# Attention work of a hybrid transformer block regrouped: logits of four jobs at once, placed with the value products between two token tiles, and query and key turning moved from TensorE to DMA transposes

## The chip, the cores and the metric

The program runs on one core of one Trainium2 chip. The metric is the device time of one execution in microseconds (us), taken as the median of several; lower is better.

## The reference, cut to what matters

One layer on 256 tokens of width 1024, all in float32: a mixer with three attention branches, then a SwiGLU FFN.

```python
h, mem_n = rms_norm(x, pre_mix_g), rms_norm(mem, mem_norm_g)
(q_n, k_c, v_c, k_s, v_s, k_w, v_w, g_n, q_m, k_m, v_m, q_x,
 gate_nsa, gate_moba, gate_mem) = split_columns(h @ w_in)          # 2328 + 3 x 1024 columns
# NSA, 8 heads of 64 in 2 groups: keys compressed to 15, "selected" blocks, a window, each gated
o_nsa = gb[..., 0:1] * o_c + gb[..., 1:2] * o_s + gb[..., 2:3] * o_w
o_m = moba_attention(q_m, k_m, v_m, rel_bias)                      # 4 heads, causal
o_x = memory_attention(q_x, *split(mem_n @ w_mem_kv))              # 4 heads into 256 memory tokens
merged = (sigmoid(gate_nsa) * (o_nsa @ w_nsa_o) + sigmoid(gate_moba) * (o_m @ w_moba_o)
          + sigmoid(gate_mem) * (o_x @ w_mem_o))
x = x + rms_norm(merged @ w_mix_out, post_mix_g)
h = rms_norm(x, pre_ffn_g)
x = x + rms_norm((silu(h @ w_ffn_gate) * (h @ w_ffn_up)) @ w_ffn_down, post_ffn_g)
```

At 256 tokens every selected block is chosen, so the selected and the window branch are both causal attention with their own keys. That makes 4 MoBA heads, 4 memory heads, 8 selected and 8 window heads: 24 score matrices of 256 x 256, of which all but the memory ones are causal (the first token tile sees 128 keys, the second 256).

## The kernel before

**Projections.** Tokens lie in two tiles t = 0 and 1 of 128. A weight matrix comes in by parts of 256 rows x 512 columns, numbered v. SyncE loads units of two parts into four `raw` buffers; ScalarE (ACT) rounds a part into `wh` (L577, counted by `hi_done`), VectorE (DVE) takes the rest into `wl` (L888, `lo_done`), and TensorE (PE) multiplies it in `sub`: for each t, for each of two 128-row halves, three matmuls of 512 columns (L1271, L1272, L1273: high x high, high x low, low x high), 12 in all. Four parts make a block b, which accumulates in one half of the PSUM tile `acc` (b % 2). Before a block begins, `free_acc(b)` waits until both token tiles of block b - 2 have been read out: `ev[0]` and `ev[1]` at b - 1 or more, increments that come block by block.

**Front.** Blocks 0 to 5 give queries, keys and values (`pat`), and the memory's (`kvm`). Matmuls need queries and keys with the head dimension on partitions, so `qk_batch` turns four 128 x 128 tiles by TensorE transposes (L1384) into a PSUM bank, and ACT copies the bank out (`evac_qk`, L664). There are eight batches: 0 is the input of the compression, 1 to 3 the NSA queries and keys, 4 and 5 MoBA's, 6 the memory keys, 7 the memory queries (in slot 0). They stand between parts of blocks 2 to 5.

**Attention.** Slots n = 0 to 27 follow, one part v = V_GATE + n of a gate or output projection each, so that the projection covers the attention. Slots 0 to 15 hold gate blocks 6 to 9; slots 16 and 17 are blocks 10 and 11 (MoBA's output projection, one part each); slots 18 to 21 are block 12; slots 22 and 23 are blocks 13 and 14 (the memory's); slots 24 to 27 are block 15. The 24 jobs are n = 0 to 3 MoBA, 4 to 7 memory, then by fours selected, selected, window, window for heads i and 4 + i. A job goes through all engines:

- PE, `scores(n)` (L1464) at the start of an even slot: logits of jobs n and n + 1, one on array rows 0 to 63, the other on rows 64 to 127, in float32 (two records per matmul), into two of three banks.
- DVE: bias added (L1105), row maxima (L1113), `x_done` (L1115).
- ACT: `exp` with the sum (L761), `e_done`. DVE: reciprocal (L1125), `r_done`.
- GpSimd (POOL): scales the job in `sx` (L529), splits it into 16-bit halves `pplanes` (L535). `sx` and `pplanes` hold two jobs each.
- SP: `cross_probs(n)` turns them by a DMA transpose (L440) into `pcrossed`, also two jobs deep (it waits for `joined`). ACT: `join` (L738) in slot n + 3 puts the halves together.
- PE, `values(g)` (L1504): four joined jobs times values into bank `ob`, at the end of slots 7, 11, 15, 19, 23 and 27, so right ahead of the next `scores`. ACT then takes `ob` to `oh` (L745) and DVE the rest to `ol` (L1142).

ACT and DVE run a written order. In slot n, ACT does: high part of v = V_GATE + n + 5 or so, exp of job n, `join(n - 3)`, `oh`, and where a gate block has ended its read-out (`evac_gate`, L723; block 12's is in its slot 21). DVE does: maxima of job n, then the read-out of an output block (`merge`, L1079; block 10 in its slot 17, block 13 in its slot 23), the low part, the reciprocal of job n, `ol`. Slot 4 also holds four TensorE transposes of the compressed probabilities (L1525), which ACT copies to `pct` (L752).

After slot 27 come the NSA projection (blocks 16, 17), the mix, and 11 FFN blocks and the down projection, which the change leaves alone.

## Time and profile before

| | |
|---|---|
| median of 3 runs | 402.14 us (401.96 to 402.21) |
| profiled execution, its own time | 402.37 us |
| its span (first to last instruction) | 400.6 us |
| PE, DVE, ACT, POOL busy | 98%, 66%, 61%, 24% |
| attention slots 0 to 27 | from 77 to 179 us of the span |

Times in rows are microseconds from the start of the span, unless marked ns. Durations of matmuls are modelled latencies that overlap; the distance from the start of one to the start of the next is the cost. PE is TensorE's matmuls, SPq the issue of a DMA by SyncE.

### The profile page before, as it was taken

What the parts mean: (1) busy time and instruction counts of PE and PEld (TensorE: products, weight loads), DVE (VectorE), ACT (ScalarE), POOL (GpSimd) and SP (SyncE); (2) the same over time, 40 slices, a digit from 0 to 9 for tenths busy, and PEclk for the clock granted to TensorE, in tenths of its full rate; (3) what the DMA queues carried; (4) which work ended last, traced back from release to release, by engine and by line L of the source; (5) the groups of instructions that cost most, each with busy time, mean ns of one, the idle gap of its engine ahead of it and who ended that gap; (6) DMA issues with size and microseconds to landing.
All of it is one profiled execution on the core that took longest, in us unless ns stands there. A gap on an engine that the chain in (4) does not pass through costs nothing.

```text
span 400.6 us, 5611 instructions
## 1 busy us (share of the span) xinstructions
PE 392.8 (98%) x1950; PEld 315.9 (79%) x1950; DVE 264.8 (66%) x438; ACT 244.3 (61%) x410; POOL 94.3 (24%) x127
## 2 busy tenths in 40 slices
PE   8999999999999999999999999999999999999994
PEld 5788888877777777778888888888888888888883
DVE  4876764897697898957769673566556566556424
ACT  5675673559999988755548853545554546444422
POOL 3100010045856455310000032133333321210000
PEclk9999999999999999999999999999999999999998
DMA  8999994655998978968564584677778777865002
GB/s 284 392 378 393 317 369 164 211 144 147 236 306 196 239 165 200 230 214 290 184 209 153 192 259 131 211 204 199 213 222 236 231 191 183 222 224 207 2 1 105
DMA packets 84784, 86.68 MB, mean 216 GB/s; under 512 B 33948, under 2 KB 61128, under 8 KB 84760
## 3 DMA queue, kind: packets, MB, share of 16 engines
q1 hardware_dynamic: 83384, 83.49, 69.9%
q0 software_dynamic: 800, 2.33, 1.7%
q10 hardware_dynamic: 576, 0.56, 0.4%
q8 instruction: 13, 0.21, 0.2%
q14 instruction: 11, 0.09, 0.1%
HBM read 77.43 MB, written 1.07 MB: 196 GB/s over the span
## 4 chain that ended last, share of the span: by engine, by line
PE 88%; ACT 3%; DVE 3%; issue 2%; POOL 2%; DMA 1%; DVEq 0%; ACTq 0%; SPq 0%; POOLq 0%
PE acc L1271 25%; PE acc L1273 25%; PE acc L1272 25%; PE ob L1504 2%; DMA gates<-pplanes 1%; PE ptb L1434 1%; PE acc L1316 1%; ACT sx L761 1%; PE acc L1312 1%; PE acc L1575 1%; PE acc L1576 1%; PE acc L1317 1%; PE acc L1581 1%; POOL pplanes L535 1%; ACT pts L738 1%
## 5 line engine op out<-in xcount | busy, mean ns | idle before, releaser
L888 DVE TENSOR_TENSOR wl<-raw,wh 128x1024 fp32r<-128x1024 f32 (+1 forms) x126 | 159.0, 1271 | 84.5 <-ACT wh L577 84.0
L577 ACT ACTIVATE wh<-raw 128x1024 fp32r<-128x1024 f32 (+1 forms) x126 | 130.1, 1044 | 68.9 <-PE acc L1273 66.1
L1271 PE MATMUL acc<-wh,xlh 128*128 128x512 f32 (+1 forms) x352 | 137.5, 391 | 0.0
L1273 PE MATMUL acc<-wh,xlh 128*128 128x512 f32 (+1 forms) x352 | 135.5, 385 | 0.0
L1272 PE MATMUL acc<-wl,xlh 128*128 128x512 f32 (+1 forms) x352 | 135.5, 385 | 0.0
L1271 PEld LDWEIGHTS acc<-wh,xlh 128*128 128x128 f32 x352 | 66.1, 188 | 15.8 <-issue 3.2
L1273 PEld LDWEIGHTS acc<-wh,xlh 128*128 128x128 f32 x352 | 66.1, 188 | 13.4
L1272 PEld LDWEIGHTS acc<-wl,xlh 128*128 128x128 f32 x352 | 66.1, 188 | 12.5
L555 POOL COPY at<-crossed 128x512 uint16<-128x512 uint16 x22 | 22.8, 1084 | 80.8 <-DMA crossed<-planes 80.8
L1271 PE MATMUL acc<-wh,ah 128*128 128x512 f32 x88 | 34.2, 389 | 0.0
L1272 PE MATMUL acc<-wl,ah 128*128 128x512 f32 x88 | 34.2, 389 | 0.0
L1273 PE MATMUL acc<-wh,al 128*128 128x512 f32 x88 | 34.2, 389 | 0.0
L535 POOL COPY pplanes<-sx 128x768 uint16<-128x768 uint16 (+1 forms) x24 | 25.4, 1056 | 8.0 <-DMA gates<-pplanes 7.0
L761 ACT ACTIVATE sx<-sx,jst 128x128 f32<-128x128 f32 (+1 forms) x40 | 17.9, 448 | 8.1 <-DVE jst L1115 7.7
L837 ACT ACTIVATE glu<-acc,rstd 128x256 f32<-128x256 f32 x22 | 10.4, 475 | 16.5 <-PE acc L1273 16.5
L529 POOL TENSOR_SCALAR sx<-sx,jst,gsig 128x128 f32<-128x128 f32 (+1 forms) x32 | 15.8, 505 | 19.3 <-DVE jst L1125 19.3
L1271 PEld LDWEIGHTS acc<-wh,ah 128*128 128x128 f32 x88 | 16.5, 188 | 3.5
L1272 PEld LDWEIGHTS acc<-wl,ah 128*128 128x128 f32 x88 | 16.5, 188 | 3.5
L1273 PEld LDWEIGHTS acc<-wh,al 128*128 128x128 f32 x88 | 16.5, 188 | 3.4
L738 ACT ACTIVATE pts<-gates 128x768 uint16<-128x768 uint16 (+1 forms) x16 | 17.7, 1109 | 0.0
L550 POOL COPY planes<-glu 128x1024 uint16<-128x1024 uint16 x11 | 12.4, 1125 | 20.0 <-DVE glu L1220 20.0
L529 POOL TENSOR_SCALAR sx<-sx,jst 128x256 f32<-128x256 f32 (+1 forms) x16 | 10.2, 649 | 29.1 <-DVE jst L1125 29.1
(198 smaller groups left out, 444.8 us busy)
## 6 DMA issues: line engine op xcount, KB each, us to landing
raw<-in_w_in SPq DMA_DIRECT2D x18, 1024.0 KB
raw<-in_w_ffn_gate SPq DMA_DIRECT2D x22, 512.0 KB
raw<-in_w_ffn_up SPq DMA_DIRECT2D x22, 512.0 KB
raw<-in_w_ffn_down SPq DMA_DIRECT2D x22, 512.0 KB
raw<-in_w_mix_out SPq DMA_DIRECT2D x4, 1024.0 KB
raw<-in_w_mem_kv SPq DMA_DIRECT2D x2, 1024.0 KB
raw<-in_w_nsa_o SPq DMA_DIRECT2D x2, 1024.0 KB
tb<-g_scratch SPq DMA_DIRECT2D x1, 1536.0 KB, 11.2
```

The source lines that it names most:

```text
L529: ins = nc.gpsimd.tensor_scalar(probs, probs, jst[:, 3, n, t:t + 1], branch_gate, ALU.mult, ALU.mult)
L535: nc.gpsimd.tensor_copy(pplanes[:, n % 2, 0:2 * w].rearrange("p (h c) -> p h c", h=2), sx[:, n % 2, 0:w].bitcast(U16).rearrange("p (c h) - ...
L550: nc.gpsimd.tensor_copy(planes[:], act_tok.bitcast(U16).rearrange("p t (n h) -> p h t n", h=2)).then_inc(planes_done, 1)
L555: ins = nc.gpsimd.tensor_copy(at[:, j].bitcast(U16).rearrange("p f (t n h) -> p h t f n", t=TILES, h=2)[:, h], crossed[:, h])
L577: nc.scalar.activation(wh[:, k, :, 0:w], raw_part(slot, part)[:, :, 0:w], ACT.Copy).then_inc(hi_done, 1)
L738: ins = nc.scalar.activation(dst.bitcast(U16).rearrange("p (c h) -> p h c", h=2), src, ACT.Copy)
L761: ins = nc.scalar.activation(probs, src, ACT.Exp, bias=jst[:, 1, n, t:t + 1], scale=SCALE, accum_out=jst[:, 2, n, t:t + 1])
L837: nc.scalar.activation(silu[:, t], acc[:, j, t, 0:GU_W], ACT.Silu, scale=rstd[:, 3, t:t + 1]).then_inc(silu_done, 1)
L888: nc.vector.tensor_tensor(wl[:, k, :, 0:w], raw_part(slot, part)[:, :, 0:w], wh[:, k, :, 0:w].bitcast(F32), ALU.subtract).then_inc(lo_done, 1)
L1271: nc.tensor.matmul(bank[:, 0:w], h[:, k, c], wh[:, slot, s, 0:w], start=first, stop=False)
L1272: nc.tensor.matmul(bank[:, 0:w], h[:, k, c], wl[:, slot, s, 0:w], start=False, stop=False)
L1273: return nc.tensor.matmul(bank[:, 0:w], l[:, k, c], wh[:, slot, s, 0:w], start=False, stop=last)
```

## The change

1. Query and key tiles of batches 1, 2, 3, 6 and 7 (now `QK_PAIRS` k = 0 to 4), and the compressed probabilities (`CMP_TURN`, k = 5), are no longer turned by TensorE. POOL splits a pair of tiles into 16-bit halves (`split_qk`), SP turns them by a DMA transpose (`cross_qk`), POOL joins them with two copies (`join_qk`). ACT's copies out of PSUM for them are gone. The batch of the compression (`compress_turn`) and MoBA's two (`moba_turn`) stay on TensorE.
2. Logits come for four jobs at once (`group_scores`), except for the memory jobs, which keep pairs (`pair_scores`). For the NSA groups one matmul takes selected and window keys together, 256 or 512 columns wide. The t = 0 logits of four jobs lie in bank 2, the t = 1 logits in banks 0 and 1. Row halves 0 and 1 of the array do unlike tiles at a time.
3. `values(g)` and `group_scores(n)` stand after the t = 0 matmuls of the part in slots 0, 8, 12, 16, 20 (values alone in slot 24), in place of the end or start of slots. The last `values` stays after slot 27.
4. `sx` becomes a ring of four (two of them in `gates`); ACT's exp and DVE's bias addition wait for POOL's split of job n - 4. DVE computes maxima of job n + 1 in slot n, after the reciprocal, except for the first job of a group. ACT's and DVE's read-out of `ob` moves to slots 8, 12, ..., 24.

The diff, cut to its core:

```diff
+QK_PAIRS = [("q", Q_NSA), ("q", Q_NSA + 2), ("k", K_SEL), ("k", K_MEM), ("q", Q_MEM)]
+QK_READY = [1, 1, 3, 5, 6]
+QK_NSA_Q, QK_ALL = 2, 5
...
+def values_group(slot):
+    if slot == JOBS + VALUE_LAG - 1:
+        return JOBS // 4 - 1
+    return slot // 4 - 2 if slot % 4 == 0 and slot >= 8 else None
...
@@ SP
+            def cross_qk(k):
+                sp.wait_ge(qk_split, k + 1)
+                sp.dma_start_transpose(qk_buffers[QK_BUFFER[k]][1].rearrange("p (b n) -> p b n", n=P),
+                                       qk_buffers[QK_BUFFER[k]][0]).then_inc(qk_turned[QK_BUFFER[k]], 16)
...
             projection(3)
+            cross_qk(0)
+            cross_qk(1)
...
             sp.dma_start(tb[:], ...)
+            cross_qk(2)
             for u in range(2 * B_GATE, 2 * B_GATE + 5):
                 mix_unit(u)
+                if u >= 15:
+                    cross_qk(u - 12)
             cross_probs(0)
             mix_unit(17)
             cross_probs(1)
             cross_probs(2)
+            cross_qk(CMP_TURN)
...
@@ POOL
+            split_qk(0)
+            split_qk(1)
+            pool.wait_ge(cmp_in_done, 1)
             nc.gpsimd.memset(vcz, 0.0).then_inc(zeroed, 1)
+            join_qk(0)
+            join_qk(1)
+            split_qk(2)
             pool.wait_ge(tb_d, 16)
...
+            join_qk(2)
+            pool.wait_ge(mq_pe, 2)
             nc.gpsimd.memset(pcz, 0.0).then_inc(zeroed, 1)
+            split_qk(3)
+            split_qk(4)
+            join_qk(3)
             for n, (kind, *_r) in enumerate(jobs):
+                if n == CMP_SLOT - 2:
+                    join_qk(4)
+                if n == CMP_SLOT - 1:
+                    split_qk(CMP_TURN)
+                if n == CMP_SLOT + 2:
+                    join_qk(CMP_TURN)
                 pool.wait_ge(r_done, n + 1)
...
@@ DVE
             for n in range(JOBS + VALUE_LAG):
+                if n < JOBS and (n % 4 == 0 or in_pairs(n) and n % 2 == 0):
+                    row_maxima(n)
...
                     nc.vector.reciprocal(jst[:, 3, n, :], jst[:, 2, n, :]).then_inc(r_done, 1)
+                    if n % 2 == 0 or n % 4 == 1 and not in_pairs(n):
+                        row_maxima(n + 1)
...
@@ PE
+            def group_scores(n):
+                if n == 0:
+                    pe.wait_ge(mq_ev, 2)
+                    pe.wait_ge(cmp_read, 1)
+                elif in_pairs(n - 1):
+                    pe.wait_ge(e_done, n)
+                else:
+                    pe.wait_ge(x_done, n)
+                if n == 0:
+                    steps = [(0, 0), (1, 1), (2, 0), (3, 1), (0, 1), (1, 0), (2, 1), (3, 0)]
+                    for i, (j, t) in enumerate(steps):
+                        if i == 5:
+                            pe.wait_ge(even_firsts, 1)
+                        ins = logits_of(n + j, t)
+                        if i == 2:
+                            ins.then_inc(even_firsts, 1)
+                else:
+                    logits_of(n, 0, keys=2).then_inc(even_firsts, 1)
+                    logits_of(n + 1, 1, keys=2)
+                    logits_of(n, 1, keys=2)
+                    pe.wait_ge(even_firsts, n // 4)
+                    ins = logits_of(n + 1, 0, keys=2)
                 ins.then_inc(s_done, 1)
...
             for n in range(JOBS + VALUE_LAG):
-                if n < JOBS and n % 2 == 0:
-                    scores(n)
-                if n == CMP_SLOT:
...
+                if in_pairs(n) and n % 2 == 0:
+                    pair_scores(n)
+                def attention(n=n):
+                    g = values_group(n)
+                    if g is not None and n < JOBS + VALUE_LAG - 1:
+                        values(g)
+                    if n < JOBS and n % 4 == 0 and not in_pairs(n):
+                        group_scores(n)
...
-                    gate_sub(n)
-                if n == 0:
-                    qk_batch(QK_LAST, 6, [col(C_QX), col(C_QX + P)])
-                if n >= VALUE_LAG + 3 and n % 4 == 3:
-                    values((n - VALUE_LAG - 3) // 4)
+                    gate_sub(n, attention)
+                if n == JOBS + VALUE_LAG - 1:
+                    values(JOBS // 4 - 1)
```

`pair_scores(4)` waits for `qk_joined` at 5 and `x_done` at 4, `pair_scores(6)` for `e_done` at 5; `compressed_scores` waits for `qk_joined` at 2.

## Rows read from the trace of the kernel before

**Rows 1.** The page: busy time of each engine, and the granted TensorE clock by slices.
```profile
PE 392.8 (98%) x1950; PEld 315.9 (79%) x1950; DVE 264.8 (66%) x438; ACT 244.3 (61%) x410; POOL 94.3 (24%) x127
...
PEclk9999999999999999999999999999999999999998
```

**Rows 2.** Windows: start:end, length, busy of each engine, PEclk, DMA share, GB/s.
```profile
30.00:54.00 24.00, 24.00 (x115) 19.85 (x114) 17.21 (x24) 15.81 (x26) 0.53 (x1) 1.00 1.06 356
98.00:106.00 8.00, 7.51 (x48) 5.80 (x47) 6.16 (x11) 7.90 (x19) 7.82 (x7) 1.00 0.92 211
```

**Rows 3.** Timeline of PE around batch 2: start, duration, engine, line, operation.
```profile
37.73 0.39 PE L1273 MATMUL acc<-wh,xlh 128*128 128x512 f32 x1
37.96 0.60 PE L1384 MATMUL sbank<-const,pat 128*128 128x128 f32 x4
38.31 0.48 PE L1271 MATMUL acc<-wh,xlh 128*128 128x512 f32 x1
38.63 0.40 PE L1272 MATMUL acc<-wl,xlh 128*128 128x512 f32 x1
```

**Rows 4.** Timeline of PE around `scores(2)`.
```profile
82.69 0.39 PE L1273 MATMUL acc<-wh,xlh 128*128 128x512 f32 x1
83.01 0.37 PE L1464 MATMUL ptb<-kt,qt 64*128 64x128 f32 x1
83.02 0.37 PE L1464 MATMUL sbank<-kt,qt 64*128 64x128 f32 x1
...
83.34 0.38 PE L1464 MATMUL ptb<-kt,qt 64*128 64x256 f32 x1
...
83.56 0.38 PE L1464 MATMUL ptb<-kt,qt 64*128 64x256 f32 x1
...
83.87 0.50 PE L1271 MATMUL acc<-wh,xlh 128*128 128x512 f32 x1
84.20 0.39 PE L1272 MATMUL acc<-wl,xlh 128*128 128x512 f32 x1
```

**Rows 5.** Timeline of PE: the transposes of slot 4, behind scores.
```profile
90.60 0.66 PE L1525 MATMUL ob<-const,pat 128*128 128x128 f32 x4
91.02 0.48 PE L1271 MATMUL acc<-wh,xlh 128*128 128x512 f32 x1
```

**Rows 6.** Timeline of PE: the last product, then `values(0)`; the same, then `values(1)`.
```profile
103.05 0.39 PE L1273 MATMUL acc<-wh,xlh 128*128 128x512 f32 x1
103.93 1.52 PE L1504 MATMUL ob<-pts,pat 128*64 128x256 f32 x16 [0.49 <-issue]
...
118.11 0.39 PE L1273 MATMUL acc<-wh,xlh 128*128 128x512 f32 x1
119.07 1.08 PE L1504 MATMUL ob<-pat,kvm 128*64 128x256 f32 x8 [0.57 <-ACT pts L738]
```

**Rows 7.** Timeline of PE and DVE after `scores(16)`.
```profile
136.73 0.50 PE L1271 MATMUL acc<-wh,oh 128*128 128x512 f32 x1
...
136.85 0.62 DVE L1105 TENSOR_TENSOR sx<-sbank,tb 128x128 f32<-128x128 f32 x2
...
140.97 1.28 DVE L1079 SCALAR_TENSOR_TENSOR gates<-gates,acc 128x512 f32<-128x512 f32 x2
```

**Rows 8.** Timeline of PE, ACT and DVE after `scores(20)`.
```profile
151.66 0.50 PE L1271 MATMUL acc<-wh,xlh 128*128 128x512 f32 x1
...
157.77 1.25 ACT L723 ACTIVATE gates<-acc,rstd 128x512 f32<-128x512 f32 x2
...
162.47 1.28 DVE L1079 SCALAR_TENSOR_TENSOR gates<-gates,acc 128x512 f32<-128x512 f32 x2
```

**Rows 9.** One line each: durations in ns, and landing of the transposes, min/median/max.
```profile
L555 POOL COPY at<-crossed x22: 763/777/1743, 237.5 to 352.3; 128x512 uint16<-128x512 uint16 x22
...
DMA to landing us min/median/max: 2.7/4.2/6.5
```

**Rows 10.** The line of POOL that splits jobs: durations in ns, min/median/max.
```profile
L535 POOL COPY pplanes<-sx x24: 824/825/1974, 81.2 to 166.6; 128x768 uint16<-128x768 uint16 x20, 128x1024 uint16<-128x1024 uint16 x4
```

More of the change, by code:

```diff
@@ L102, in job_plan, with in_pairs, sx_place, sx_user @@
     return jobs
+def in_pairs(job):
+    return MOBA_H <= job < MOBA_H + MEM_H
+def sx_place(job):
+    return job % 4 if job < JOBS - 2 else job % 2
+def sx_user(job):
+    return job - 4 if job < JOBS - 2 else job - 2
+def logits_count(job):
+    g = job // 4
+    return 1 if g == 0 else 2 + job % 4 // 2 if g == 1 else g + 2
 def ends_group(job):
@@ L242, in build_layer @@
             jst = sb("jst", [P, 5, JOBS, TILES], F32, s)
+            with ExitStack() as early:
+                front = sb("front", [P, 2, 1024], U16, early)
+            qk_buffers = [(front[:, 0], front[:, 1]),
+                          tuple(pts[:, j].rearrange("p t q -> p (t q)").bitcast(U16) for j in (2, 3)),
+                          tuple(gates[:, j, 5 * SLICE:6 * SLICE].bitcast(U16) for j in range(2))]
+            sx_ring = [sx[:, 0], sx[:, 1], gates[:, 0, 0:SLICE], gates[:, 1, 0:SLICE]]
             pplanes = sb("pplanes", [P, 2, 1024], U16, s)
@@ new lines, in row_maxima @@
+            def row_maxima(n):
+                kind, h, _q, _k, bh = jobs[n]
+                dve.wait_ge(s_done, logits_count(n))
+                if kind == "mem":
+                    bank = score_banks[n % 4 % 3]
+                    link(nc.vector.tensor_reduce(jst[:, 0, n, :], bank.rearrange("p (t k) -> p t k", t=2), AX, ALU.max))
+                else:
+                    if n >= 4:
+                        dve.wait_ge(pplanes_done, sx_user(n) + 1)
+                    for t in range(TILES):
+                        c0, c1 = prob_cols(kind, t)
+                        nc.vector.tensor_tensor(prob_view(n, kind, t), logits(n, t), tb[:, bh, c1 - c0 - 1::-1],
+                                ALU.add).then_inc(dve_c, 1)
+                        chain[0] += 1
+                    dve.wait_ge(dve_c, chain[0] - 1)
+                    for t in range(TILES):
+                        if t == 1:
+                            dve.wait_ge(dve_c, chain[0])
+                        ins = nc.vector.reduce_max(jst[:, 0, n, t:t + 1], prob_view(n, kind, t), axis=AX)
+                    link(ins)
+                nc.vector.tensor_scalar(jst[:, 1, n, :], jst[:, 0, n, :], -SCALE, None, ALU.mult).then_inc(x_done, 1)
@@ L1451, in scores, with logits_of @@
-            def scores(n):
-                if n == 0:
-                    pe.wait_ge(qk_ev[1], 3)
-                    pe.wait_ge(qk_ev[0], 4)
-                elif jobs[n - 2][0] == "mem":
+                        after={0: [lambda: moba_turn(0)], 1: [lambda: moba_turn(1)], 2: [compress_1], 3: [add_column_groups]})
+            whole_block(B_TAIL, 20, 4, xh, xl, w=ATT_TAIL, after={1: [compress_2], 3: [compressed_scores]})
+            def logits_of(n, t, keys=1):
+                _kind, _h, q, k, _bh = jobs[n]
+                rows, dst = half_rows(n % 2), logits(n, t)
+                count = dst.shape[1]
+                if keys == 2:
+                    c = 256 * (n % 2) if t == 0 else 0
+                    dst = score_banks[2 if t == 0 else n % 2][:, c:c + 2 * count].rearrange("p (a c) -> p a c", a=2)
+                    return nc.tensor.matmul(dst, qt[rows, q, P * t:P * t + P], kt[rows, k:k + 2, 0:count], start=True, stop=True)
+                return nc.tensor.matmul(dst, qt[rows, q, P * t:P * t + P], kt[rows, k, 0:count], start=True, stop=True)
@@ L1457, in scores, with pair_scores @@
+            def pair_scores(n):
+                if n == MOBA_H:
+                    pe.wait_ge(qk_joined, QK_ALL)
+                    pe.wait_ge(x_done, n)
+                else:
                     pe.wait_ge(e_done, n - 1)
-                else:
-                    pe.wait_ge(x_done, n - 1)
                 for t in range(TILES):
                     for side in range(2):
-                        kind, _h, q, k, _bh = jobs[n + side]
-                        c0, c1 = prob_cols(kind, t)
-                        ins = nc.tensor.matmul(score_banks[(n + side) % 3][:, c0:c1], qt[half_rows(side), q, P * t:P * t + P],
-                                               kt[half_rows(side), k, 0:c1 - c0], start=True, stop=True)
+                        ins = logits_of(n + side, t)
+                ins.then_inc(s_done, 1)
@@ L1488, in values @@
                 pe.wait_ge(joined, 4 * g + 4)
-                if g == 0:
-                    pe.wait_ge(te_done, 1)
+                if jobs[4 * g][0] == "sel":
+                    pe.wait_ge(qk_joined, CMP_TURN + 1)
                 sides = [[], []]
```

205 lines of the change are left out of this document (100 added, 105 removed).

## The prediction, written before the run

> **What bounds the kernel now.** I read the page first, then the timeline of PE, then the order of DVE and ACT in the attention slots. The page shows PE busy 98% of the span at the full granted clock, the other engines at most 66% [rows 1]. So a thing that leaves PE's queue is worth its time, as long as nothing else makes PE wait. Busy time of PE hides short waits, since the durations are latencies that overlap. I therefore measure from start to start: products follow each other every 0.23 us [rows 3], and whatever widens that distance is a cost.
>
> Three costs show. Four transposes between products: 38.63 - 37.73 less two pitches of 0.23 is 0.44 us [rows 3]. A pair of logits by the same sum: 84.20 - 82.69 - 0.46 = 1.05 us, of which entering takes 0.32 - 0.23 = 0.09, the products behind it come 0.11 late, and the rest is from 83.01 to 83.87 [rows 4]. Last, waits at `values`: its first record comes 0.88 us behind the last product for group 0 and 0.96 for group 1 [rows 6], against 0.32 for an entry that waits for nothing [rows 4], so 0.56 + 0.64 = 1.20 us are stall. In that stretch ACT is busy 7.90 of 8 us and POOL 7.82 [rows 2]: the chain over the other engines is late there, not PE.
>
> **What leaves PE.** (a) Transposes. Batches 1, 2, 3 and 7 stand alone: 4 x 0.44 = 1.76 us. Batch 6 shares its excursion with `compress_2` and slot 4's with scores; four transposes are 0.42 us there [rows 5], so 0.84. Sum 2.60.
>
> (b) Grouping. A 256-column record pair takes 83.56 - 83.34 = 0.22 us a record [rows 4]; two records of it and two half as wide make 0.64 us for a pair of jobs of 128 + 256 columns, the rest of the 1.05 is entry, exit and fill, 0.41. Four jobs have twice the columns: 1.28 + 0.41 = 1.69 us alone. Wide matmuls with two keys have the same columns. Slots 10, 14, 18 and 22 lose an excursion of 1.05, and 0.64 of it returns in the group ahead (which stands behind `values` before and after): 4 x 0.41 = 1.64. MoBA's two pairs cost 0.86 (scores 0 shares an excursion with the compressed scores, so only 83.87 - 83.01) + 1.05 = 1.91, its group 1.69: 0.22. Memory pairs stay. Sum 1.86.
>
> (c) Stalls of `values` 0 and 1: they come 6 products or 1.4 us later in PE's order, and the jobs come earlier, since DVE does the maxima of job n + 1 in slot n, `sx` is four deep, and ACT loses the copy of batch 7 and of `pct`. I take the whole 1.20. With none of it the gain is 1.2 less; that is the lower end of this term.
>
> Together 2.60 + 1.86 + 1.20 = 5.66 us.
>
> **What PE meets in place of it.** In DVE's order nothing of slot n goes ahead of the maxima of a group's first job, and they need `s_done`. After that moment DVE and ACT need a fixed time for what lies in their queues, and some of it is what `free_acc` waits for. The trace shows these times, and the change shortens PE's way to those waits.
>
> - Slot 18 (block 12) waits for `merge` of block 10, in DVE's slot 17: queued ahead of it are the maxima of 16, a low part, the reciprocal, the maxima of 17. Before, PE's next product after scores(16) is at 136.73 and the merge ends at 140.97 + 1.28 = 142.25, 5.5 us later [rows 7]. PE had the whole of slots 16 and 17 and a pair of logits to do until then and lost nothing. After, only 6 + 12 products lie between: 18 x 0.23 + 0.11 = 4.25 us. Stall 1.3 us.
> - Slot 23 (block 14) waits for ACT's read-out of block 12 in its slot 21, behind exp 20, join 17, `oh`, a high part, exp 21 and join 18: it ends at 157.77 + 1.25 = 159.02, 7.4 us after 151.66 [rows 8]. PE is there after 30 products, 7.0 us. Stall 0.4 us.
> - Slot 24 (block 15) waits for `merge` of block 13, DVE's slot 23, behind exp 22 on ACT and the maxima of 23: 162.47 + 1.28 = 163.75, 12.1 us after 151.66 [rows 8]. PE is there 7.4 + 12 x 0.23 = 10.1 us after. Before, scores(22) and `values(4)` (now inside slot 24, behind the wait) filled this time. Stall 2.0 us.
>
> Sum 3.7 us. Behind a stalled `free_acc` stand all later products; the high and low parts are several parts ahead, so nothing else is late. The stalls don't pay each other back: each is counted from its own `s_done`. Had DVE and ACT been quicker by 2 us everywhere, nearly all would vanish, so the term runs from 0 to 3.7; three POOL clashes of 0.7 us more (below) give 5.8.
>
> **What the other queues get.** POOL gets six splits and six joins. A join is two copies like those of L555, 0.78 us each, 1.74 at most [rows 9], so 1.6 to 3.5 us; a split of 1024 half-words is like L535's, 0.8 to 2.0 us [rows 10]. Most lie where POOL does little (0.53 of 24 us in the windows [rows 2]). The tight one is `join_qk(4)`: it stands ahead of job 2 on POOL, and `pair_scores(4)` on PE waits for it. From the end of MoBA's group PE has 42 products, 9.7 us, to go to it. In that time DVE does the maxima of jobs 0 and 1 and a low part, ACT two exps, POOL scales and splits jobs 0 and 1 (before, a job took it 1.8 us) and joins: about 6.8 + 1.6 = 8.4 us as an estimate, or 9.7 and more if low parts of DVE get in first. So 0 to 1 us of stall, I take 0.3. `join_qk(5)` delays jobs 6 and 7, which `values(1)` needs; laying the same durations end to end, they are joined less than 1 us ahead of PE, an estimate with no margin to speak of. POOL's longest splits take 1.97 us against a median of 0.83 [rows 10]. The Trainium skill ("SBUF — State Buffer", Who interferes with whom) says that a VectorE instruction with two SBUF inputs and a GpSimd instruction that reads SBUF shut each other out for a whole instruction, the later one waiting; the trace agrees with its 1.97 against 0.83, and by it each clash costs up to one low part on either side.
>
> SP issues `cross_qk(0)` and `(1)` behind part 7's load, with DMA at a share of 1.06 [rows 2], so loads for blocks 4 and 5 land later by two issues and two turns, an estimate of 5 us from landings of 2.7 to 6.5 us [rows 9]. The rounding of those parts runs 4 us or more ahead of PE. Cost 0; if that cover is gone, 1 to 2 us. ACT only loses work in front.
>
> **The sum.** 5.66 - 3.7 - 0.3 = 1.7 us. The profiled execution took 402.37 (span 400.6 and 1.8 around it), which gives 400.7; it lies 0.2 above the median of 402.14, which gives 400.4.
>
> **The rivals.** They and my forecast share 100.
>
> 1. Stalls don't appear (18): the read-outs are earlier, the gain is 4.5 to 5.6 and the time 396.5 to 397.6. For it: the ring of four frees DVE and ACT from POOL. Against: both long chains are ACT's and DVE's own work after `s_done`, as measured.
> 2. Tiles of unlike length on the two row halves do not run side by side (8): slower. Before, both halves start together (83.01 and 83.02 [rows 4]) but always with equal columns; the groups set 256 columns beside 512. Run one by one the four matmuls take 2.56 us in place of 1.28, in five groups 6.4 us: 5.66 - 3.7 - 6.4 = -4.4, so 406.6. It decides from 0.35 us lost a group. The Trainium skill ("TensorE: Matmul & The Clock Gate", The mechanism) says that matmuls keep program order in start and in end, and tiles on other row groups still overlap. By that rule the written order, short, long, long, short, would still overlap in full, and the sum stays; if order also held each matmul's two records together, part of the 6.4 would come.
> 3. POOL and the turns become the bound of slots 4 to 12 (18): `qk_joined`, `joined` 4 or 8 come late, PE keeps its stalls at `values` and gets new ones of 1 to 2 us. Gain 1.7 - 1.2 - 1.5 = -1.0, so 401 to 403.5. For it: POOL 7.82 of 8 us busy before it got more. Against: all jobs start their chain with PE further behind them.
> 4. Turns starve the front of weights (4): 402 to 404.
>
> My forecast has 52.
>
> **How the numbers follow.** A measurement of this kernel can tell about 0.2% (0.8 us) from no change. Within my case, 399.0 to 401.8, some 8 of 52 are above 401.3. Faster: 44 + 18 = 62. Same: 8 + 8 of rival 3. Slower: 10 + 8 + 4 = 22. The range leaves out rival 2, the lowest of rival 1 and the highest of 3 and 4: 397.2 to 403.2.
>
> **What would show it.** Distances between products at former batches 1, 2, 3 and 7 of 0.23; `values` 0 and 1 entered 0.32 behind a product; the group's records from first to last about 1.3 us; PE records pausing before slots 18, 23 and 24 by 1.3, 0.4 and 2.0 us, with `merge` ending 5.5 and 12.1 us after the group. It is wrong if those pauses are missing (faster), if the group takes over 1.6 us, or if PE pauses at `pair_scores(4)` or `values(1)` (slower).

## The result, and the profile after

The changed kernel takes 402.89 us, the median of 6 runs (402.24 to 404.13); the kernel before, on the same chip, takes 402.17 (401.96 to 402.64, 6 runs). The ratio is 1.0022, with an interval of 1.0012 to 1.0031: slower by 0.2%. I had predicted 400.4. The profiled execution took 402.24 with a span of 400.4 us, which makes it the fastest of the six; before, the profiled one had a span of 400.6.

The page of the kernel after, in the lines of [rows 1]:

```profile
PE 388.7 (97%) x1894; PEld 314.1 (78%) x1894; DVE 266.7 (67%) x438; ACT 240.3 (60%) x404; POOL 121.5 (30%) x146
...
PEclk9999999999999999999999999999999999999998
```

PE has 56 records fewer and 4.1 us less of busy time, and the span is 0.2 us shorter. So the work did leave PE, and something made PE wait for as long. POOL has 27 us more. The windows of [rows 2] for the kernel after (start:end, length, busy of each engine, PEclk, DMA share, GB/s):

```profile
30.00:54.00 24.00, 24.00 (x112) 19.88 (x111) 19.65 (x26) 13.93 (x23) 7.01 (x7) 1.00 1.08 315
98.00:106.00 8.00, 8.00 (x48) 5.96 (x47) 5.12 (x9) 7.07 (x16) 7.87 (x9) 1.00 0.88 208
```

In the second stretch, which holds `values(0)` in both kernels, ACT and DVE got free by about a microsecond each; POOL is as full as before. Where PE waited, in the list of its waits from 30 to 200 us (in all, how often, longest):

```profile
PE acc L1380 <- DVE gates L1181: 2.7, 2, 1.6
PE acc L1380 <- ACT gates L828: 0.8, 1, 0.8
PE ob L1638 <- ACT pts L843: 0.7, 1, 0.7
PE sbank L1563 <- DVE jst L1217: 0.4, 1, 0.4
```

The first two lines are the read-outs before slots 18, 24 and 23 (L1181 is `merge`, L828 `evac_gate`), the third is `values(1)`, the fourth `pair_scores(4)`. The first of them on PE, and the merge that ends it on DVE (the timelines of both, after the group of slot 16):

```profile
135.16 0.50 PE L1380 MATMUL acc<-wh,oh 128*128 128x512 f32 x1
...
139.17 0.39 PE L1382 MATMUL acc<-wh,ol 128*128 128x512 f32 x1
140.72 0.47 PE L1380 MATMUL acc<-wh,xlh 128*128 128x512 f32 x1 [1.17 <-DVE gates L1181]
...
139.35 1.27 DVE L1181 SCALAR_TENSOR_TENSOR gates<-gates,acc 128x512 f32<-128x512 f32 x2
```

The merge ends at 140.62, 5.46 us behind the product after the group; [rows 7] gave 5.5. PE comes from 139.17 to 140.72 in 1.55 us where 0.23 is the pitch: 1.32 us of stall (a stall is here a gap between two starts, less 0.23 ahead of a product and 0.32 ahead of an excursion, that is, of logits or `values` between products). Measured so, slot 23 has a gap of 1.14 (0.91 stall) and slot 24 one of 1.95 (1.72 stall), the merge of block 13 ending at 163.40, 12.3 us after 151.07. The sum is 3.95 us. Behind each of the three the next product follows by 0.31 in place of 0.23, another 0.25 us in all.

The whole account, each number a distance between starts of products:

| | predicted | measured |
|---|---|---|
| transposes off PE | 2.60 | 2.2: all left, but at `compress_2` 0.4 of it became a wait |
| grouping | 1.86 | 1.81: four excursions of 1.05 gone, `values` with a group 0.63 longer than `values` with a pair; MoBA's two pairs cost 0.77 + 1.05, its group 1.70 |
| stalls of `values` 0 and 1 gone | 1.20 | 0.40: 0.56 gone at `values(0)`, 0.64 became 0.80 at `values(1)` |
| read-outs, slots 18, 23, 24 | 1.3 + 0.4 + 2.0 | 1.32 + 0.91 + 1.72, and 0.25 behind them |
| `pair_scores(4)` | 0.3 | 0.47 |
| net gain | 1.7 | -0.2 |

One distance checks the sum: from the last product ahead of the first transposes (31.32 before, 31.03 after) to the first product of the NSA projection (178.73 and 178.57) PE needs 147.41 us before and 147.54 after, 0.1 us more. That the span is 0.2 us shorter all the same comes from the 0.3 us by which that first product is earlier, which is no part of any term. The median lies another 0.65 above the profiled execution.

The group of slot 8, ahead of it `values(0)`, behind it the next product; the two row halves write to `ptb` (256 columns) and `sbank` (512):

```profile
103.92 0.48 PE L1562 MATMUL ptb<-kt,qt 64*128 64x256 f32 x1
103.92 0.69 PE L1562 MATMUL sbank<-kt,qt 64*128 64x512 f32 x1
104.24 0.38 PE L1562 MATMUL ptb<-kt,qt 64*128 64x256 f32 x1
104.45 1.02 PE L1562 MATMUL sbank<-kt,qt 64*128 64x512 f32 x3
104.89 0.59 PE L1562 MATMUL ptb<-kt,qt 64*128 64x256 f32 x2
105.41 0.50 PE L1380 MATMUL acc<-wh,xlh 128*128 128x512 f32 x1
```

From its first record to the next product it takes 1.49 us, with twice the columns of a pair, which took 0.86 [rows 4].

### The profile page after: what moved, and what is told of

It is laid out like the page before. It is cut to its first block, busy times and chain, and to the rows that moved or that the text cites. A ratio compares the mean times of both kernels' runs of the same rounds, so it can differ in the third digit from the quotient of the medians.

```text
span 400.4 us, 5514 instructions
## 1 busy us (share of the span) xinstructions
PE 388.7 (97%) x1894; PEld 314.1 (78%) x1894; DVE 266.7 (67%) x438; ACT 240.3 (60%) x404; POOL 121.5 (30%) x146
## 3 DMA queue, kind: packets, MB, share of 16 engines
HBM read 77.43 MB, written 1.07 MB: 196 GB/s over the span
## 4 chain that ended last, share of the span: by engine, by line
PE 83%; DVE 6%; POOL 5%; DMA 2%; ACT 2%; issue 1%; DVEq 0%; ACTq 0%; POOLq 0%
PE acc L1380 24%; PE acc L1382 24%; PE acc L1381 23%; PE ob L1638 2%; POOL gates L637 2%; POOL pplanes L643 2%; DMA gates<-pplanes 1%; DVE wl L989 1%; PE acc L1421 1%; PE acc L1425 1%; POOL sx L637 1%; DVE jst L1215 1%; DMA gx<-in_gx 1%; PE acc L1707 1%; PE acc L1708 1%
## 5 line engine op out<-in xcount | busy, mean ns | idle before, releaser
L989 DVE TENSOR_TENSOR wl<-raw,wh 128x1024 fp32r<-128x1024 f32 (+1 forms) x126 | 159.6, 1278 | 84.9 <-ACT wh L685 84.5
L1382 PEld LDWEIGHTS acc<-wh,xlh 128*128 128x128 f32 x352 | 66.1, 188 | 13.3
L663 POOL COPY at<-crossed 128x512 uint16<-128x512 uint16 x22 | 24.8, 1172 | 80.2 <-DMA crossed<-planes 80.2
L643 POOL COPY pplanes<-sx 128x768 uint16<-128x768 uint16 (+1 forms) x14 | 16.1, 1148 | 3.0 <-DMA gates<-pplanes 2.3
L637 POOL TENSOR_SCALAR sx<-sx,jst,gsig 128x128 f32<-128x128 f32 (+1 forms) x20 | 10.9, 558 | 15.0 <-DVE jst L1231 15.0
L863 ACT ACTIVATE sx<-sx,jst 128x128 f32<-128x128 f32 (+1 forms) x24 | 10.7, 447 | 6.4 <-DVE jst L1217 6.4
L1380 PE MATMUL acc<-wh,oh 128*128 128x512 f32 x32 | 12.9, 403 | 0.8 <-ACT gates L828 0.8
```

Source lines behind the costliest of these rows:

```text
L637: ins = nc.gpsimd.tensor_scalar(probs, probs, jst[:, 3, n, t:t + 1], branch_gate, ALU.mult, ALU.mult)
L643: nc.gpsimd.tensor_copy(pplanes[:, n % 2, 0:2 * w].rearrange("p (h c) -> p h c", h=2), sx_ring[sx_place(n)][:, 0:w].bitcast(U16).rearrange ...
L663: ins = nc.gpsimd.tensor_copy(at[:, j].bitcast(U16).rearrange("p f (t n h) -> p h t f n", t=TILES, h=2)[:, h], crossed[:, h])
L863: ins = nc.scalar.activation(probs, src, ACT.Exp, bias=jst[:, 1, n, t:t + 1], scale=SCALE, accum_out=jst[:, 2, n, t:t + 1])
L989: nc.vector.tensor_tensor(wl[:, k, :, 0:w], raw_part(slot, part)[:, :, 0:w], wh[:, k, :, 0:w].bitcast(F32), ALU.subtract).then_inc(lo_done, 1)
L1380: nc.tensor.matmul(bank[:, 0:w], h[:, k, c], wh[:, slot, s, 0:w], start=first, stop=False)
```

## The experiments

The runs were made on three chips, and each ratio is against the kernel before on the same chip, whose median lies between 402.12 and 402.30 there. Waits and stalls are those of the one profiled execution of each kernel, which is not always a typical one: it was the slowest of its kernel's runs in e3, e5 and e8, the second slowest in e4 and e7, and the fastest in e2 and e6.

**e1_turn_alone.** Only the DMA turning; pairs of logits, a ring of two and `values` stay where they were.

```diff
-    return job % 4 if job < JOBS - 2 else job % 2
+    return job % 2
...
-                if in_pairs(n) and n % 2 == 0:
-                    pair_scores(n)
+                if n < JOBS and n % 2 == 0:
+                    scores(n)
```

> Part 1 alone: queries, keys and compressed probabilities turned by DMA, logits in pairs, one order of DVE and ACT, two-deep sx and values as in the kernel before. Theory POOL (GpSimd's chain of splits, joins and jobs sets when values 0 and 1 can begin): PE loses 2.6 us of transposes, but the waits ahead of values 0 and 1 grow by as much or more, from 1.2 us to 3.5 us or more; the time is 402 to 404 us. Rival (GpSimd's new work is hidden): the waits stay near 1.2 us and the time is 399.6 to 400.5 us. No pause before slots 18, 23 and 24 in either.

Measured: 401.56 us (401.14 to 404.02, 12 runs), ratio 0.999 (0.9978 to 1.0001). PE's waits in this kernel:

```profile
PE ob L1604 <- ACT pts L835: 1.6, 2, 0.8
PE sbank L1551 <- ACT sx L855: 0.7, 1, 0.7
```

No read-out is waited for. Both `values` wait 0.80 and 0.91 us, against 0.56 and 0.64 before, and the pair of slot 6 waits 0.80. So turning is worth its 2.2 us on PE and gives back 0.24 + 0.27 + 0.80 of them through jobs that come late: 0.9 us are left, and the span is 399.4 against 400.6 (the first excursion is 0.2 us earlier). Neither expectation came true as written: the two `values` wait 1.7 us together, not 3.5 nor 1.2, and the time lies between the two ranges. The wait of `values(1)` stands at the end of the same chain here as in the kernel before: POOL's split of job 8 (1.9 us in both), for which, with `sx` two deep, DVE's bias addition of job 10 waits, then the exponential of job 10 on ACT, then the join of job 7.

**e2_group_alone.** Grouping, placement and the ring of four, with every transpose on TensorE as before. The edit is the other half of the same diff.

> Parts 2 to 4 alone: grouped logits and values between token tiles, ring of four, TensorE transposes and ACT's copies as in the kernel before. Theory READ-OUT (after a group's logits DVE and ACT need a fixed time until they free the accumulator that slots 18, 23 and 24 want, and PE has too little to do meanwhile): the three pauses are there, 3.5 to 4 us together; with 1.9 us of logits saved and the waits ahead of values 0 and 1 gone or nearly gone (GpSimd has no splits and joins) the time is 401.8 to 403.2 us. Rival (the pauses come from GpSimd's new work, which also slows DVE): the pauses are under 1 us together and the time is 399 to 400 us.

Measured: 404.62 us (404.14 to 408.59, 6 runs), ratio 1.0089 (1.0058 to 1.012).

```profile
PE acc L1323 <- DVE gates L1124: 2.7, 2, 1.6
PE acc L1323 <- ACT gates L766: 0.7, 1, 0.7
PE sbank L1512 <- DVE jst L1160: 0.5, 1, 0.5
PE ob L1609 <- DVE pat L1186: 0.2, 1, 0.2
```

The three pauses are here in full (1.33, 0.91, 1.71) though POOL has nothing more to do than before. They belong to parts 2 to 4, that is, to the grouping and its placement. `values` 0 and 1 are entered in 0.32 us: without the six splits, turns and joins the stalls do vanish, as I had expected of the whole change. The time is 1.4 us above the expected range: from the first excursion to the NSA projection PE needs 2.1 us more than before. The expectation left out `pair_scores(4)` (0.57 of stall), a wait for the compressed probabilities (0.2) and the 0.25 behind the pauses. With the grouping in place the turning is worth 1.7 us (404.62 against 402.89), alone 0.6.

**e3_readout_early.** The changed kernel with the three read-outs ahead of work that doesn't wait for them: `merge` of block 10 in DVE's slot 16, directly behind the reciprocal (it was in slot 17), `merge` of block 13 in slot 22 ahead of the low part (it was in 23), and ACT's `evac_gate` of block 12 ahead of the exponential of 21.

```diff
+                    if n == SLOT_MOBA:
+                        merge(B_MOBA)
...
+                if n == SLOT_MEM:
+                    merge(B_MEM, low=False)
...
+                if n - 3 == SLOT_GATE_NSA[0]:
+                    act.wait_ge(pplanes_done, n - 1)
+                    evac_gate(B_GATE_NSA[0], V_GATE + n)
```

> The changed kernel, with the read-outs of blocks 10 and 13 on DVE and of block 12 on ACT moved ahead of the maxima and exp that stood before them. Theory READ-OUT: the pauses before slots 18, 23 and 24 (3.9 us in the profile) fall under 0.5 us, and the time to 398.9 to 399.8 us. Rival (PE's early arrival is taken back by the next wait, values 4 or 5 or the joins): the pauses turn up elsewhere and the time stays above 401.5 us.

Measured: 398.86 us (398.47 to 400.7, 6 runs), ratio 0.9913 (0.99 to 0.9925). The waits:

```profile
PE ob L1644 <- ACT pts L843: 1.4, 1, 1.4
PE sbank L1569 <- DVE jst L1219: 0.4, 1, 0.4
```

The pauses are gone and the median is 4.0 us lower. In the profile PE needs 144.05 us from the first excursion to the NSA projection, 3.5 less than in the kernel after: the pauses gave 4.2 back, and `values(1)` waits 1.44 in place of 0.80. So the place of three short instructions in the queues was the whole cost of the pauses.

**e4_cmp_late.** The changed kernel with the last turn (the compressed probabilities) split, turned and joined in jobs 9 to 12, so that POOL has less ahead of job 7.

```diff
-                if n == CMP_SLOT - 1:
+                if n == CMP_SLOT + 5:
                     split_qk(CMP_TURN)
-                if n == CMP_SLOT + 2:
+                if n == CMP_SLOT + 8:
                     join_qk(CMP_TURN)
```

> The changed kernel, with the split, turn and join of the compressed probabilities moved on GpSimd from jobs 3 and 6 to jobs 9 and 12. Theory POOL: GpSimd is busy without a gap from 89.6 to 111 us and 3 us of it are this work, so values 1 no longer waits (0.8 us less) and the time is 401.8 to 402.4 us, with less spread. Rival (the wait at values 1 is SP's order or ACT's): the wait stays at 0.6 us or more and the time at 402.6 to 403.2 us.

Measured: 402.41 us (402.17 to 402.91, 11 runs), ratio 1.0006 (0.9998 to 1.0015). The stall at `values(1)` stayed, 1.12 us in the profile. POOL had the planes of job 7 ready at 107.2, but SyncE issued their turn at 109.59, when ACT's join of job 5 was done, and it landed 6.8 us later at 116.4. So POOL's row was not the last thing that decides. The median is at the edge of Theory POOL's range and 0.5 us under the changed kernel's, with less spread; as the profiled execution was a slow one of its kernel, the profile can't say whether the stall was shorter in the others. Two causes were left: the join of job 5 behind an exponential that waits for the group, or the transfer itself.

**e5_join_first.** On top of e3: in slots 8, 12, 16 and 20 ACT joins job n-3 ahead of the exponential of n.

```diff
+                early = n % 4 == 0 and 8 <= n < JOBS
+                if early:
+                    join(n - JOIN_LAG)
```

> On top of the version with the early read-outs (398.86 us, stall of values(1) 1.44 us there): in slots 8, 12, 16 and 20 ScalarE does the join of job n-3 ahead of the exponential of job n, which waits for the group's logits. Theory A (the turn of job 7 is issued late, because SyncE waits for the join of job 5 and that join sits behind the exponential of job 8): the join of job 5 ends some 2 us earlier, the turn of job 7 with it, the stall of values(1) falls from 1.44 to under 0.5 us, and the time by about 1 us, to 397.8. Theory B (VectorE's and GpSimd's chain, that is the planes of job 7, sets it): stall 1.4 as before, time 398.9. Theory C (the exponentials of jobs 8 and 12 come later by a join of 1.3 us and their chain is the tight one): the stall moves on to values(2) or to the pauses, time 399 to 400.

Measured: 399.42 us (398.28 to 400.06, 5 runs), ratio 0.9919 (0.9906 to 0.9931): no gain over e3. The stall is 1.63, and a pause of 0.72 came back before slot 18, as Theory C had it in part. Here job 7's planes were ready at 111.13, and the join of job 5 had not been in their way; the turn took 5.83 us to land. With POOL as late as this, Theory A has nothing to act on.

**e6_split_later.** The text below speaks of the changed kernel, but the kernel that ran stands on e3, so its baseline is 398.86 and not 402.89. One wait is added on POOL.

```diff
+            pool.wait_ge(cmp_dve, 3)
             split_qk(3)
             split_qk(4)
```

> The changed kernel with one added wait: GpSimd's split of the memory keys (1.04 us) starts after VectorE's multiplies of the hidden layer. Theory A (the split shares a port with VectorE and stretches the multiply at L1128 to 1.09 us, for which compress_2 waits): that multiply is 0.2 us again, the gap at compress_2 goes from 1.12 to about 0.75 us, the time falls by 0.35 to 402.5. Rival: GpSimd comes later by about 1 us and stays behind until slot 12, since it is busy without a break from 89.6 us: the stall of values(1) grows from 0.8 to about 1.8, time 403.5.

Measured: 398.04 us (397.56 to 398.81, 4 runs), ratio 0.9898 (0.9884 to 0.9913), span 395.8: 0.8 us less than e3's median (0.6 by the ratios, since the chips differ). In the kernel after, the timelines of DVE and POOL around `compress_2` read

```profile
65.58 0.21 DVE L1127 COPY hx<-ob 128x60 f32<-128x60 f32 x1
65.83 1.08 DVE L1128 TENSOR_TENSOR hx<-hx 128x60 f32<-128x60 f32 x1
66.95 0.19 DVE L1129 TENSOR_SCALAR hx<-hx 128x60 f32<-128x60 f32 x1
...
65.80 1.04 POOL L595 COPY pts<-kvm 128x1024 uint16<-128x1024 uint16 x1 [0.79 <-DVE kvm L1085]
```

and in e6

```profile
66.06 0.22 DVE L1130 TENSOR_TENSOR hx<-hx 128x60 f32<-128x60 f32 x1
...
67.93 1.47 POOL L595 COPY pts<-kvm 128x1024 uint16<-128x1024 uint16 x1 [2.89 <-DVE hidv L1138]
```

A multiply of 60 columns takes 1.08 us when POOL's copy starts 0.03 us before it, and 0.22 when it does not; the gap at `compress_2` falls from 1.12 to 0.72. That is the exclusion that the Trainium skill ("SBUF — State Buffer", Who interferes with whom) describes, and the trace agrees: the multiply ends within 0.07 us of the copy. The stall of `values(1)` is 0.57 here against 1.44 in e3, since its turn landed in 4.74 us and not in 5.62; POOL handed it over at the same distance from `values(0)` as in e3 (8.34 us), so the added wait did not cause this.

**e7_ahead_of_part.** The changed kernel with `values` and group logits ahead of the part instead of between its tiles.

```diff
+                attention()
                 if n in (SLOT_MOBA, SLOT_MOBA + 1):
...
-                    gate_sub(n, attention)
+                    gate_sub(n)
```

> The changed kernel with values and group logits ahead of the part instead of between its two token tiles: both come six products (1.4 us) earlier against the stream. Theory A (the pauses before slots 18, 23 and 24 are the lateness of VectorE's and ScalarE's chain behind the group of slot 16 and 20): they shrink by 1.4 each, from 1.32, 0.91 and 1.72 to 0, 0 and 0.3, together by 3.6. What it costs: if GpSimd's row sets the turn of job 7, the stall of values(1) grows from 0.8 to 2.2, and values(2) may start to wait; time 402.9 - 3.6 + 1.4 = 700.7 less 300, that is 400.7. If instead the join of job 5 behind the exponential of job 8 sets it, group 8 is also 1.4 earlier and the stall stays 0.8: 399.3. Rival (the place within the part is worth nothing, since every chain is as late as the group): 402.9.

Measured: 402.06 us (399.64 to 403.52, 12 runs), ratio 0.999 (0.9974 to 1.0006). All three pauses and the wait of `pair_scores(4)` are gone, 4.4 us: group and read-outs both come six products earlier, while slots 18, 23 and 24 stay. But `values(1)` now waits 2.89 us, and group 0 waits 0.9 for the compressed scores to be read. And behind both waits the granted clock fell to 0.50, that is 1.2 of 2.4 GHz (windows of this kernel: start:end, length, busy of PE, PEld, DVE, ACT, POOL, PEclk, DMA share, GB/s; then PE):

```profile
75.00:76.00 1.00, 0.32 (x2) 0.35 (x4) 0.94 (x4) 0.00 (x0) 0.71 (x1) 0.55 0.21 46
76.00:78.00 2.00, 2.00 (x15) 1.88 (x14) 0.58 (x1) 1.35 (x2) 1.07 (x3) 0.50 1.12 340
...
120.00:122.00 2.00, 1.96 (x10) 1.33 (x12) 1.17 (x2) 1.73 (x6) 0.43 (x1) 0.50 1.15 296
```

```profile
116.83 0.39 PE L1382 MATMUL acc<-wh,xlh 128*128 128x512 f32 x1
120.04 1.97 PE L1638 MATMUL ob<-pat,kvm 128*64 128x256 f32 x8 [2.82 <-ACT pts L843]
121.78 1.60 PE L1638 MATMUL ob<-pts,kvm 128*64 128x256 f32 x8
```

Eight matmuls of `values` take 1.74 us here and 0.88 at the full clock (2.4 GHz). In the account: 4.4 gained, 2.1 lost at `values(1)`, 1.4 to its clock, 2.1 at group 0 (wait and clock), so about 1.0 us more than in the kernel after, and the first excursion is 0.3 us later; the span is 401.7 against 400.4. But this was a slow execution (403.51). The median is 402.06 with a spread of 3.9 us, 0.8 us below the changed kernel's, and the intervals of the two ratios do not overlap. So in most runs the place between the tiles earned nothing: it gives each `values` 1.4 us more and takes the same 1.4 us from the read-outs.

**e8_all.** e3, e4, e5 and e6 together.

> Early read-outs, the join first in slots 8 to 20, the compressed probabilities' planes at jobs 9 to 12, and the memory keys' split behind VectorE's multiplies. If each reason holds: pauses of 3.9 us gone, stall of values(1) 0 to 0.3, compress_2 without its 0.35: 402.9 - 3.9 - 0.8 - 0.35 = 397.8; against the early read-outs alone (398.9) that is 1.1 less. Rival (the moved work on GpSimd and ScalarE only moves the waits to values(2) and values(3)): 398.9 or more.

Measured: 397.62 us (397.08 to 397.73, 4 runs), ratio 0.9877 (0.9863 to 0.9891), the lowest median of all, 5.3 us under the changed kernel; the interval overlaps e6's, and the spans are 395.9 and 395.8. The time is the expected one, the reasons are only in part: the pauses and the 0.4 at `compress_2` are gone, but the stall of `values(1)` is 0.74 and not 0 to 0.3. The end of its chain (start, length):

```profile
107.80 7.75 DMA gates<-pplanes
115.56 0.02 issue
115.58 1.37 ACT pts L845
```

The turn of job 7 is issued 3 us earlier than in the kernel after and lands at 115.55, against 115.79 there and 115.36 in e6. An earlier issue bought nothing: the transfer now takes 7.75 us instead of 4.97.

**e9_split_only.** The changed kernel itself, with e6's wait alone.

> The changed kernel itself (the run before it, e6, stood on the version with the early read-outs) with one added wait: GpSimd's split of the memory keys starts after VectorE's multiplies of the hidden layer. In e6 the gap at compress_2 was 0.72 us. Theory A: here it goes from 1.12 to 0.72 as well, and the rest of the stream, pauses of 3.9 us included, stays: span 400.4 - 0.4 = 400.0, time 402.5. Rival (GpSimd's lateness carries through to the turn of job 7): stall of values(1) over 1.2 us, time 403 or more.

Measured: 403.06 us (401.86 to 405.37, 12 runs), ratio 1.003 (1.0012 to 1.0047). The gap at `compress_2` is 0.72, as expected; the time did not fall. In its profile the turn of job 7 took 5.82 us:

```profile
110.79 5.82 DMA gates<-pplanes
116.61 0.02 issue
116.63 1.36 ACT pts L844
```

Its planes were ready at 110.77, where the kernel after has 110.80, and the same transfer took 0.85 us longer; the stall is 1.62 against 0.80, and so the 0.4 gained at `compress_2` is gone twice over. The rival's numbers came true (a stall over 1.2 us, 403 or more), but not by its reason: POOL was not later.

**e10_turn_ahead.** On top of e6: the turn of job 7 is issued ahead of the weight piece that stood before it.

```diff
-                elif n in (6, 7):
+                elif n == 6:
                     mix_unit(14 + n)
...
                 cross_probs(n)
+                if n == 7:
+                    mix_unit(21)
```

> On top of e6 (398.04 us, stall of values(1) 0.57): the turn of job 7 is issued ahead of the weight piece of 1 MB in two loads that stands before it in SyncE's queue, instead of 2.4 us after it. Theory A (the turn lands when the transfers queued ahead of it are through: it landed at 115.4 to 116.4 in every version, whether issued at 107.8, 109.6 or 110.6): it lands at least 1 us earlier, the stall is 0, time 397.5. Theory B (the turn is bound by its own work of about 4.7 us, the load ahead of it shares nothing that counts): landing 4.7 us after issue, stall as before, time 398.0. Rival: the weight piece, now 2.5 us later, starves TensorE four slots on: a wait on a piece of weights of up to 2 us appears, time 399 or more.

Measured: 398.6 us (398.35 to 400.24, 6 runs), ratio 0.9921 (0.9906 to 0.9937). The stall of `values(1)` fell from 0.57 to 0.22: the turn was no longer last, and ACT was busy until it joined at 114.90. The turn itself was issued at 110.34 and landed at 113.42, after 3.1 us in place of 4.7: 1.9 us earlier than in e6, from an issue 0.3 us earlier. So Theory A holds for the landing. But the weight piece now stands ahead of the turn of job 8 together with the next one. That turn was issued at 113.25, 1.6 us behind the first of the two pieces, and took 7.7 us. The turns of this kernel from 104 to 122 us, of which those two are the shortest and the longest:

```profile
DMA to landing us min/median/max: 3.1/5.4/7.7
```

POOL, which waits for the turn of job 8, sat idle until 121.10

```profile
121.10 0.82 POOL L646 COPY pplanes<-gates 128x768 uint16<-128x768 uint16 x1 [4.14 <-DMA gates<-pplanes]
```

and `values(2)`, which no version had made wait, was entered 1.33 us late. The wait moved with the piece of weights. The rival had it as a wait for the weights themselves, and that did not come.

**e11_turn_split.** e1 with e6's wait.

> The turning alone (e1: 401.56 us, gap at compress_2 1.12) with the split of the memory keys behind VectorE's multiplies. Theory A (the gain is local to compress_2): gap 0.72, time 401.2. Rival (GpSimd is the bound of jobs 4 to 7 here, stalls of 0.80 at the pair of slot 6, 0.80 at values(0) and 0.91 at values(1) in e1, and starts 1 us later): these grow by up to 1 us, time 401.6 to 402.5. It also says what grouping and placement are worth with the early read-outs, against e6 (398.04).

Measured: 401.56 us (400.85 to 402.21, 11 runs), ratio 0.9983 (0.9974 to 0.9992). The gap at `compress_2` is 0.72; the pair of slot 6 waits 1.11 instead of 0.80: the gain is used up there. Against e6 (398.04) it shows what grouping and placement are worth once the read-outs are moved: 3.5 us.

## Why the prediction was wrong

**What held.** The transposes left PE at batches 1, 2, 3 and 7. A group cost 1.70 us against 1.69, so tiles of unlike length on the two row halves run side by side (one after the other, at 0.11 and 0.22 us a record, those of group 0 would take an estimated 2.6 us and not 1.51), and the second rival is refuted; the Trainium skill's rule ("TensorE: Matmul & The Clock Gate", The mechanism) had said so for the order as written, and the trace agrees, 1.82 us from product to product over the whole group. The pauses before slots 18, 23 and 24 came where they were expected, 3.95 us against 3.7, from the times between `s_done` and the read-outs in [rows 7, 8]; e2 shows that they belong to the grouping, and e3, which moves only the read-outs, gets them back. The first rival is refuted by the same.

**Where it failed: term (c).** "I take the whole 1.20" was wrong for `values(1)`: it waits 0.80 us after the change, more than the 0.64 before. I had set the new work of POOL against the head start of the jobs as "less than 1 us ahead of PE, an estimate with no margin to speak of", and then booked the margin as a gain. What the runs showed in its place: the old chain did go, and another one took over. Before, the wait ended a chain through the ring of two (e1 above), and the ring of four cuts it. After, the wait ends a chain of POOL (busy without a break from 89.6 us), one transfer and a join. Its last pieces in the kernel after:

```profile
106.75 2.95 POOL gates L637 x2
109.70 0.05 issue
109.75 1.05 POOL pplanes L643
110.80 0.02 issue
110.82 4.97 DMA gates<-pplanes
115.78 0.02 issue
115.81 1.37 ACT pts L843
```

The first piece scales job 7; the same two instructions took 0.94 us for job 6. While they ran, DVE made two low parts (L989) from 106.78 to 109.34. In e4 and e8, where POOL reached job 7 earlier, the scaling took 0.93. So 2 us of this chain are a clash of the kind that I had named, and term (c) holds nothing for it. Such a clash is not new (before, the scaling of job 5 took 3.03), but now it falls on the last job of the group; no run moved it alone. (I had compared 1.97 us with 0.83; those are copies of 1024 and of 768 half-words, and the undisturbed copy of 1024 takes 1.04. A clash costs such a copy about 1 us.)

e2, without POOL's splits and joins and without their turns, has no such stall. Taking work from POOL (e4, e8) or from ACT's queue (e5) does not remove it either, because the transfer then takes longer or POOL hands over no earlier. Counted from the start of `values(0)` in each profile:

| | turn of job 7 issued | behind the last load by | landed | took | stall of `values(1)` |
|---|---|---|---|---|---|
| after | 8.35 | 2.6 | 13.3 | 4.97 | 0.80 |
| e3 | 8.34 | 2.4 | 14.0 | 5.62 | 1.44 |
| e5 | 8.33 | 2.4 | 14.2 | 5.83 | 1.63 |
| e9 | 8.34 | 2.4 | 14.2 | 5.82 | 1.62 |
| e6 | 8.34 | 2.5 | 13.1 | 4.74 | 0.57 |
| e10 | 8.31 | 5.5 | 11.4 | 3.08 | 0.22 |
| e4 | 6.82 | 3.0 | 13.6 | 6.82 | 1.12 |
| e8 | 5.51 | 1.8 | 13.3 | 7.75 | 0.74 |

At one and the same time of issue the stall follows the transfer to 0.03 us, except in e10, where ACT was last. An issue up to 2.8 us earlier (e4, e8) does not bring the landing forward; putting the turn ahead of the piece of weights (e10) does, by 1.7 us against e6 on this scale. The 24 turns of the attention in the kernel before say the same: the 11 that were issued within 3 us of the last load ahead of them took 4.1 to 6.5 us (median 5.3), the 13 others 2.7 to 4.7 (median 2.8). The median landing of 4.2 us in [rows 9], which I had in mind, mixes the two kinds, and the turn that counts is of the slow one: 4.7 to 7.8 us. That the load delays the turn is shown for e10 alone, as the only run that changed their order and nothing else.

**Term (a)** was mis-sized by 0.4: at `compress_2` PE gains the four transposes and waits for DVE's multiply, stretched by the memory keys' split on POOL. I had named the exclusion for the low parts and not looked for a short DVE instruction on the path. **`pair_scores(4)`** is 0.47 against 0.3; DVE's maxima of job 3 end at 87.50 us and POOL's `join_qk(4)` at 87.47, too close to call. e2, which has no `join_qk(4)`, waits 0.57 there for DVE's maxima alone, so POOL is not needed for the wait.

**The read-outs** were 0.25 too low: slot 23 cost 0.5 more than forecast, slot 24 0.3 less. The slower product behind each pause, 0.25 in all, I had put at nothing. **Grouping** was 0.05 too high.

Together: 0.8 (stalls of `values`) + 0.4 (`compress_2`) + 0.25 + 0.25 (read-outs) + 0.17 (`pair_scores(4)`) + 0.05 = 1.9, the difference between a net gain of 1.7 and a net loss of 0.2. Against the 400.7 that the sum gave for the profiled execution, 402.24 is 1.5 too much: the 1.9, less the 0.3 by which PE reached the first transposes earlier, to 0.1. The outcome is the third rival's (POOL and the turns bound slots 4 to 12), with smaller sizes than I gave it, since `values(0)` lost its stall all the same.

**What stays open.** The rest of the miss, 0.65 us between the profiled execution and the median, is in the spread: the six runs of the kernel after reach from 402.24 to 404.13, those before from 401.96 to 402.64, and the profiled one is the fastest of the six. In profiles of the same stretch the turn of job 7 takes 4.97 us (span 400.4) and 5.82 (e9, span 401.3), which is 0.8 us of PE's time, so the landing can make a difference of that size, and over e3 to e10 it ranges more widely still; that it makes the spread of the unprofiled runs was not shown. In e3's profile the first input (gx) also came late, with the same program up to there: ACT waited 2.78 us at the start instead of 0.27, and PE began the attention 2.1 us later (74.58 against 72.48). The change does not touch that part.

## What to carry to other kernels

When work leaves the engine that bounds a kernel, what is left between two events on it shrinks, and every wait that was covered by distance comes out. Measure, for each wait behind the change, the time from the event that starts its chain to its end, and lay the shortened distance beside it: that gave 3.7 for 3.95 us here. Then don't accept the wait: a short read-out that stands behind work with time to spare can go ahead of it, and here three such moves turned 0.2% slower into 0.9% faster. A wait can also be served by more than one chain: cutting the one that the trace of before shows (the ring of two) only shows the next.

A stall that disappears "because the others start earlier" is a gain only if the chain is followed to its last link with the durations that the crowded stretch shows, not with medians. A transfer that stands behind loads of weights has no length of its own: here it took 3.1 us with the last load 5.5 us ahead of it and 4.7 to 7.8 with one 1.8 to 3.0 us ahead, and issuing it earlier did not help. Read its length by what stands ahead of it in the queue.

## What the runs showed of the hardware that was not expected

- A turn by DMA of 128x1024 half-words (a memory job) landed after 4.97 us with a piece of weights issued 2.6 us ahead of it, 5.82 in another run of the same order (e9), 7.75 when issued 3 us earlier (e8, a piece 1.8 us ahead), and 3.08 with the piece behind it (e10).
- A DVE multiply of 128x60 with two inputs in SBUF took 1.08 us beside a copy of 128x1024 half-words on POOL and 0.22 without it (e6). Two scalings of 128x256 on POOL took 2.95 us beside DVE's low parts and 0.94 without.
- In e7 the wait of 2.82 us at `values(1)` was followed by a granted clock of 0.50, and so was one of only 0.95 us at 74.7, behind matmuls of 64x15. In e9 a wait of 1.56 us at `values(1)`, behind full products, was followed by a granted clock of 1.00. So the length of a wait alone did not tell whether the clock fell.
- Matmuls of 64x128 and 64x256 on the two row halves, started together, overlap: sixteen records from 75.92 to the next product at 77.43, 1.51 us. So do those of 64x256 and 64x512, eight records in 1.49 us.
- The product behind a pause of PE follows by 0.31 us in place of 0.23, at all three pauses.
